# Splitting each weight unit ahead of, not behind, ScalarE's side steps in a fused two-block transformer kernel

## The reference

```python
def pool_layer(x, mem, ...):        # first block, layer 0
    proj = rmsnorm(x, norm_g) @ w_in
    u, zu, qm, zm = jnp.split(proj, ...)
    y_pool = multiscale_pool(u, w_pool, pool_scale) * jax.nn.silu(zu)
    y_mem = memory_attention(qm, mem, mem_g, w_mem_kv) * jax.nn.silu(zm)
    return x + jnp.concatenate([y_pool, y_mem], axis=-1) @ w_out
# first block, layer 1: keys and values of all heads come from w_kv; blocks of 32 tokens are
# compressed by an MLP:  zb = z[:, blk] + pe ;  silu(zb @ w1) @ w2   (once for keys, once for values)
# then compressed, selected and window attention, memory attention, and @ w_out
# second block
    qkv = rmsnorm_2(x, attn_norm) @ w_qkv
    y_a = diff_attention(...)             # softmax difference of two halves, 8 heads
    y_b = stick_breaking_attention(...)   # suffix sums of log(1 - beta)
    y_c = chunk_band_attention(...)
    x = x + y @ w_o
    g = causal_dwconv(h @ w_gate, conv_w, conv_b) ; u = h @ w_up
    x = x + (jax.nn.silu(g) * u) @ w_down
    return rmsnorm_2(x, final_norm)
```

## Time and profile before

| | us |
|---|---|
| median of three runs | 2031.71 |
| lowest, highest | 2029.98, 2036.67 |
| the profiled execution | 2034.31 |
| its span, first to last instruction | 2032.5 |
| TensorE busy | 2013.9 |
| VectorE busy | 1455.5 |
| ScalarE busy | 1046.2 |
| GpSimd busy | 424.7 |
| mean granted TensorE clock | 0.997 of 2.4 GHz |

### The profile page before, as it was taken

The page is one execution under the profiler, slowest core; times in us unless marked ns, Lnnn a source line. Parts: engine busy times, 40 slices in busy tenths (PEclk is TensorE's granted clock), DMA queues, the critical chain, the costliest instruction groups (busy, mean ns, idle before and its releaser), DMA issues.

```text
span 2032.5 us, 29325 instructions
## 1 busy us (share of the span) xinstructions
PE 2013.9 (99%) x11490; PEld 1760.2 (87%) x11490; DVE 1455.5 (72%) x2056; ACT 1046.2 (51%) x1568; POOL 424.7 (21%) x395
## 2 busy tenths in 40 slices
PE   8999999999999999999999999999999999999998
PEld 7888888888888888888878888888888888888887
DVE  6866788788796556876656678777776567777755
ACT  6744544567433554644556555455454344554443
POOL 0014553300000444430222235111010000101122
PEclk9999999999999999999999999999999999999999
DMA  9664666567654334655544445566666666666664
GB/s 334 225 190 153 192 187 197 186 220 239 211 189 141 115 111 135 188 194 192 163 157 155 146 157 186 185 190 193 189 193 184 189 196 188 190 192 190 184 190 145
DMA packets 104809, 374.03 MB, mean 184 GB/s; under 512 B 11840, under 2 KB 13152, under 8 KB 104288
## 3 DMA queue, kind: packets, MB, share of 16 engines
q1 hardware_dynamic: 104384, 371.63, 57.7%
q10 hardware_dynamic: 288, 0.52, 0.1%
HBM read 370.01 MB, written 2.10 MB: 183 GB/s over the span
## 4 chain that ended last, share of the span: by engine, by line
PE 93%; DVE 3%; DMA 2%; ACT 1%; issue 0%; POOL 0%; SPq 0%; DVEq 0%; ACTq 0%
PE psg L558 50%; PE psg L559 26%; PE psg L625 2%; PE psg L627 2%; PE psg L626 2%; DVE s_w L1742 1%; DMA s_stage<-in_mk 1%; PE psg L599 1%; PE pst L599 1%; PE pst L756 1%; PE pss L847 1%; PE pst L664 1%; PE psg L602 1%; PE pso L867 1%; ACT s_w L1161 0%; PE pst L602 0%
## 5 line engine op out<-in xcount | busy, mean ns | idle before, releaser
L1742 DVE TENSOR_TENSOR s_w<-s_stage,s_w 128x1024 fp32r<-128x1024 f32 (+3 forms) x698 | 860.0, 1234 | 344.1 <-ACT s_w L1161 341.5
L1161 ACT ACTIVATE s_w<-s_stage 128x1024 fp32r<-128x1024 f32 (+3 forms) x698 | 726.7, 1043 | 715.7 <-PE psg L559 624.3
L558 PE MATMUL psg<-s_ry,s_w 128*128 128x512 f32 x2560 | 898.3, 393 | 2.9 <-DVE s_qc L1796 2.4
L559 PE MATMUL psg<-s_ry,s_w 128*128 128x256 f32 x2560 | 722.9, 282 | 0.0
L558 PEld LDWEIGHTS psg<-s_ry,s_w 128*128 128x128 f32 x2560 | 482.1, 188 | 108.8 <-issue 4.0
L559 PEld LDWEIGHTS psg<-s_ry,s_w 128*128 128x128 f32 x2560 | 485.3, 190 | 0.2
L558 PE MATMUL psg<-s_rh,s_w 128*128 128x512 f32 x1216 | 427.4, 393 | 0.3 <-DVE s_w L1742 0.3
L559 PE MATMUL psg<-s_rh,s_w 128*128 128x256 f32 x1216 | 342.7, 282 | 0.0
L558 PEld LDWEIGHTS psg<-s_rh,s_w 128*128 128x128 f32 x1216 | 228.3, 188 | 48.9 <-issue 1.0
L558 PE MATMUL psg<-s_hid,s_w 128*128 128x512 f32 x704 | 244.1, 390 | 0.0
L559 PEld LDWEIGHTS psg<-s_rh,s_w 128*128 128x128 f32 x1216 | 229.8, 189 | 0.6
(11 more groups left out here) (425 smaller groups left out, 2221.8 us busy)
## 6 DMA issues: line engine op xcount, KB each, us to landing
s_stage<-in_wo SPq DMA_DIRECT2D x96, 512.0 KB, 3.6
s_stage<-in_wg SPq DMA_DIRECT2D x84, 512.0 KB, 3.5
s_stage<-in_wu SPq DMA_DIRECT2D x84, 512.0 KB, 4.0
s_stage<-in_ain SPq DMA_DIRECT2D x64, 512.0 KB, 4.2
s_stage<-in_wd SPq DMA_DIRECT2D x64, 448.0 KB, 3.4
s_stage<-in_wkv SPq DMA_DIRECT2D x32, 512.0 KB, 3.5
s_stage<-in_wd SPq DMA_DIRECT2D x32, 512.0 KB, 3.6
s_stage<-in_bq SPq DMA_DIRECT2D x24, 512.0 KB, 3.6
```

Source lines behind the costliest of these rows:

```text
L558: e.matmul(o, M.WH[:, r, ws], xx, start=begin, stop=False)
L559: m = e.matmul(o[:, T:2 * T], M.WL[:, r, ws], xh, start=False, stop=end)
L1161: e.activation(M.weights(c, 0, n, shift), M.staged(c, n), ACT.Copy).then_inc(S["wh"], 1)
L1742: e.tensor_tensor(M.weights(c, 1, n, shift), M.staged(c, n), M.weights(c, 0, n, shift), ALU.subtract).then_inc(S["wl"], 1)
```

## The change

In ScalarE's `nxt` the two calls change places. The split of a unit is then issued ahead of ScalarE's side steps of that tick; no instruction is added or taken away, and the other four engines keep their lists. ScalarE's own `split()` calls inside the compression generator stay where they are.

```diff
@@ -1162,8 +1162,8 @@

     def nxt(n=1):
         for _ in range(n):
+            split()
             side.tick()
-            split()
```

## The result

The changed kernel takes 2066.34 us (median of four, 2064.85 to 2070.95), the kernel before 2031.89; the ratio is 1.0165, with a 95% interval of 1.0148 to 1.0182. That is 34.4 us slower. 20.8 us slower were forecast, at 2052.5, in a range from 2041 to 2068. The profiled execution took 2070.95 us with a span of 2069.2, 36.7 more than before. It was the longest of the four, so the steps inside it add up to 2.3 us more than the medians are apart.

The account below looks back on a forecast made before the run. TensorE, busy 2013.9 of 2032.5 us, was taken to bound the kernel; delays of 3.75 + 1.35 + 4.8 + 3.4 + 6.2 + 1.6 - 0.3 = 20.8 us gave 2052.5 us, range 2041 to 2068.

Parts of the forecast that it names:

- the start: First units: ScalarE's squares and columns go behind its splits, VectorE's column steps and splits come late; 3.75 us, bounds 2.0 to 4.6.
- pairs: Stick-breaking pairs: ScalarE's copy of masked logs goes behind a split, GpSimd's low part comes late four times; 6.2 us.
- heads: Differential heads: the output's high part moves behind a split, delaying GpSimd's low part of the square; eight times 0.2, 1.6 us.
- nothing happens: Rival: ScalarE is only 51% busy and the usual slack covers the delay; time stays 2031.7 us; chance 0.08.
- faster: Rival: splits freed from waiting side steps remove TensorE's waits of 6.0 us beyond the start; 2024.3 us; chance 0.02.
- Smaller: Rival: VectorE absorbs the start, GpSimd finds the copies early enough, only the compress stage pays; 9.55 us, 2041.3; chance 0.18.
- larger: Rival: five stalls drop the clock and the values stage stalls in each tick; 31.4 us, 2063.1; chance 0.17.
- the values stage: Compress, values: six ticks, VectorE's zb and splits late, a 1.13 us stall every second tick; 3.4 us, bounds 0 to 6.8.
- shift: Shift into the compress stage: ScalarE's position-bias step zb ends later, delaying VectorE at units 149 and 150; 1.35 us.
- keys: Compress, keys: five times ScalarE's zb falls between two splits, delaying VectorE; 0.91 us four times, 1.17 once; 4.8 us.
- the first delay: In the start: squares and a column behind ScalarE's splits make TensorE take unit 13 1.35 us late.
- the clock: TensorE falling to half rate behind some of the larger five stalls, 1.45 us each; 0 to 7 us, taken as 0.

Follow-up runs that it names:

- The ladder: Kernel before, with VectorE held up on purpose ahead of its split at eleven feed-forward units, for waits of about 0.5 to 3.0 us; 2062.29 us, ratio 1.0147.
- the second ladder: Kernel before, VectorE held up at the same eleven feed-forward units, with the wait lengths in another order; 2063.26 us, ratio 1.0152.

## Why the prediction was right or wrong

**The sign and the mechanism** were right. The cost lies at the named places (old order there: ratio 1.0001), and it runs over VectorE's split in the start and the compression (both first: waits for splits from 14.8 to 1.2 us) and over GpSimd in the pairs and heads. The rivals "nothing happens" and "faster" fell: the new order over 509 units is worth neither a gain nor a loss. "Smaller" fell with the pairs. The time came nearest to "larger", 2063.1, but for other reasons in part: the values stage did not stall in every tick, it stalled in every second one as forecast. The 34.4 us lie in the band given to "larger" (28 to 45, chance 0.17) and not in the forecast's own (14 to 28, 0.55), and the time is only 1.7 us inside the end of the range. Two of the signs named came out the other way. ScalarE's idle time before its splits was to fall and grew, by 258.5 us, since the split now meets the idle time first and the side steps no longer fill it. And stalls showed in the chunk-band pairs, which are attention and were counted at nothing.

**The waits** were sized well in sum. The 20.8 us were made of idle time, and PE's idle time grew by 24.1 us. Part of the agreement is luck. By place, forecast against measured, it is 3.75 and 4.7 (start), 1.35 and 1.1 (shift), 4.8 and 4.2 (keys), 3.4 and 2.6 (values), 6.2 and 6.9 (pairs), 1.6 and 3.8 (heads), and too much at three places made up for too little at three others. Single ones: unit 13 foreseen 1.35 us late, 1.0 measured, after 0.4 at unit 12; zb with the keys 0.91 against 0.84; with the values 1.13 against 0.86, 0.75 and 0.69; CU 1.5, 2.1, 2.0 and 0.6 (6.2) against 1.1, 1.9, 1.9 and 1.0 (5.9). In the start the first delay was to lie inside the second; in fact they add, 1.4 us at units 12 and 13 and 2.05 at units 19 to 21. The load at unit 9 and 0.55 us at unit 30 were not foreseen.

**What failed is the step from idle time to time lost.** The prediction charged a wait with its idle time. The ladder shows 0.27 us more for each, and the changed kernel has 29 waits more than the kernel before: 7.8 us. And it took 0 for the clock, where its own bounds went to 7. PE was at half rate in both of the first two pairs, in the first behind waits of 1.12 and 1.50 us close together, in the second behind one of 1.9, and the stretch around 647 us, which the kernel before has too after a run of small matmuls, was longer by 1.6 (mean clock over 40 us 0.87 against 0.91). At 0.21 of 8 us in each pair, 1.7 us, that makes 5.0. The sum 24.1 + 7.8 + 5.0 = 36.9 stands against 36.7 measured. By place it fits the keys (5.55 against 5.65), the pairs (11.4 against 11.05) and the heads (6.0 against 5.8). It is 1.0 too high in the start and 1.0 too low in the values, which cancel, so the last 0.2 us are luck.

```profile
1076.00:1084.00 8.00, 5.92 (x22) 0.79 0.37 121
1096.00:1104.00 8.00, 6.08 (x23) 0.79 0.21 60
```

(The changed kernel, columns as above. The stretch at 647 us is not shown to come from the change: in the other kernels with the new order at that place it moved the unit starts by anything from -1.6 to +2.6 us, and in the second ladder, which has the old order there, by +1.35.)

**Two terms were mis-sized beside that.** The differential heads, 0.2 us each, lost 0.83: 0.57 of idle time and 0.26 for the wait itself. GpSimd's output step began 0.86 us later against PE's units, because ScalarE's high part now stands behind a split, and took 0.26 us longer, because more of it fell beside a VectorE split (1.47 to 1.73 us). Together 1.12, less the 0.40 of slack that the forecast had read, is 0.72, the idle time and the 0.16 us that it doesn't show. The prediction had put an overlap as a bound on CU, where in fact there was none in the first three pairs (GpSimd took 1.82 us in the first, against 2.15 before, and 2.30 in the fourth), and not on the heads, where it was. In the first pair it followed PE's wait for GpSimd alone and missed VectorE's on the same step, worth 1.5 us. The chunk-band pairs, charged with nothing, lost 1.7 us: in the second and third GpSimd's normalisation took 4.93 instead of 3.73 us, of which its last piece took 2.13 instead of 0.92, with a VectorE split that begins 0.20 us into it (all four pieces before, then after):

```profile
1001.70 3.73 POOL L2502 TENSOR_SCALAR s_csc<-s_csc,s_stat 128x128 f32<-128x128 f32 x4 [9.18 <-DVE s_stat L2201]
```

```profile
1000.81 4.93 POOL L2502 TENSOR_SCALAR s_csc<-s_csc,s_stat 128x128 f32<-128x128 f32 x4 [8.89 <-DVE s_stat L2201]
```

It counts among what "has at least 0.9 us between ACT's step and its reader", where the slack should have been reduced by a shut-out of 1.2.

## What to carry to other kernels

Where several engines each interleave a stream of units with side work, the order on a half idle engine is not free: what counts is who waits for it in the same tick, and what stands behind that waiter. Work that needs no wait belongs ahead of the instruction that waits for a slot. When you turn stalls into time, add the price of restarting the matrix engine for each (here 0.27 us), and a chance of a clock fall, some 1.5 us, for those near 2 us and above. A gain on one link of such a chain can be lost on the next, as when VectorE split first too: the waits for splits went down by 13.6 us and the time by some 2.

## What the runs showed of the hardware

- A VectorE operation with two SBUF inputs and a two-input operation (TENSOR_TENSOR) of GpSimd exclude each other, in both directions: 8 columns on GpSimd took 1.18 us beside a split, and a VectorE step of 0.42 us (L1768) took 3.84 beside a GpSimd addition of 4.62. A VectorE step just ahead of it (L1766), with one of its two inputs in PSUM, took its 0.42 us beside the same addition. The Trainium skill (SBUF — State Buffer, SBUF: two separate sides) says that the shared pair of ports is held as an exclusive lock and that the loser blocks fully; these traces agree for these operations, with those numbers, but not for all. GpSimd's TENSOR_SCALAR L2502 of 128 x 256 takes 0.93 us alone, and a VectorE split that begins 0.43 us into it takes its usual 1.22 us (kernel before: GpSimd, then VectorE):

```profile
678.64 0.93 POOL L2502 TENSOR_SCALAR s_bsc<-s_bsc,s_stat 128x256 f32<-128x256 f32 x1
...
679.07 1.22 DVE L1742 TENSOR_TENSOR s_w<-s_stage,s_w 128x1024 fp32r<-128x1024 f32 x1
```

  The prediction had read contention as a slowing down, and said that no row isolates it; the step of 3.84 us in the trace of before does.
- Whether a 0.42 us step is caught by it looks like chance where GpSimd's start hangs on a load. GpSimd's steps there begin when a load lands. Across the eleven profiles of kernels that leave this addition as it is, that same step took 0.42 us in five, 1.9 in three and 2.85 to 3.84 in three.
- A TensorE wait costs 0.27 us beyond its shown idle time, from 0.4 to 2.85 us alike: 0.16 us by which the shown end of a matmul lies behind the start of the next in a running stream, and 0.11 us on the first matmul.
- TensorE's clock fell to its lower level, 1.2 of 2.4 GHz, in 7 of 11 waits between 1.86 and 2.85 us and in none of 11 below, for a loss of 1.3 to 1.6 us; in the first pair it fell during the second of two waits, of 1.12 and 1.50 us, that lay 3 us apart. The Trainium skill (TensorE: Matmul & The Clock Gate, Part 1) says that the granted level is one of two. The traces agree: it is 0.5 or 1.0 in every record of the thirteen profiles, and at 0.5 a wide matmul starts 0.43 us behind the one ahead of it instead of 0.23.
